# All products of 512 moving columns issued as two products of 256 columns each, bank half by bank half

## The reference

```python
def first_block(x, mem, ...):
    x = x + 0.5 * swiglu(rms_norm(x, ffn1_norm[l]), ffn1_w_in[l], ffn1_w_out[l])
    u = rms_norm(x, mix_norm[l]) @ w_in[l]
    ...
    x = x + mixed @ w_out[l]
    x = x + 0.5 * swiglu(rms_norm(x, ffn2_norm[l]), ffn2_w_in[l], ffn2_w_out[l])

def second_block(x, mem, positions, ...):
    for l in range(DEPTH_2):                 # 2 layers
        h = rms_norm_2(x, ffn1_norm_pre[l])
        x = x + 0.5 * rms_norm_2(swiglu_2(h, ffn1_w_in[l], ffn1_w_out[l]), ffn1_norm_post[l])
        h = rms_norm_2(x, mix_norm_pre[l])
        y = token_mixer(h, mem, cos, sin, ...)
        x = x + rms_norm_2(y, mix_norm_post[l])
        h = rms_norm_2(x, ffn2_norm_pre[l])
        x = x + 0.5 * rms_norm_2(swiglu_2(h, ffn2_w_in[l], ffn2_w_out[l]), ffn2_norm_post[l])
    return x
```

## Time and profile before

| | |
|---|---|
| runs | 1740.83 us median (1740.42 to 1740.84) |
| profiled execution | 1740.77 us, its span 1739.0 us |
| TensorE (PE) | busy 1729.4 us, 99%, 12568 matmuls |
| weight loads (PEld) | 1586.5 us, 91%, 12568 |
| VectorE (DVE) | 1074.9 us, 62% |
| ScalarE (ACT) | 920.5 us, 53% |
| granted TensorE clock | full, mean 1.000 |
| DMA | 189 GB/s mean |

### The profile page before, as it was taken

How to read it: one execution, slowest core, us unless ns; L and a number is a source line. 1 busy time by engine, 2 the same in 40 slices (tenths; PEclk the granted TensorE clock), 3 DMA queues, 4 the chain that set the end, 5 groups by cost and what they waited for, 6 DMA issues and landing times.

```text
span 1739.0 us, 31193 instructions
## 1 busy us (share of the span) xinstructions
PE 1729.4 (99%) x12568; PEld 1586.5 (91%) x12568; DVE 1074.9 (62%) x1516; ACT 920.5 (53%) x1265; POOL 34.4 (2%) x60
## 2 busy tenths in 40 slices
PE   9999999999999999999999999999999999999998
PEld 9999888999999999898898999899999888989997
DVE  6555787655655566556686555755584566775555
ACT  6444677444454445576746444644464576664443
POOL 0000120000000000000000000000000000000000
PEclk9999999999999999999999999999999999999999
DMA  8655524655665555553355555655555543446552
GB/s 326 244 193 193 182 109 148 227 186 196 221 228 193 187 181 200 179 212 143 122 194 188 194 190 198 231 208 195 190 201 183 194 171 128 164 157 220 192 193 96
DMA packets 47551, 328.58 MB, mean 189 GB/s; under 512 B 5488, under 2 KB 5744, under 8 KB 9072
## 3 DMA queue, kind: packets, MB, share of 16 engines
q1 hardware_dynamic: 44640, 316.93, 50.4%
q10 hardware_dynamic: 2832, 10.54, 1.7%
HBM read 326.39 MB, written 1.05 MB: 188 GB/s over the span
## 4 chain that ended last, share of the span: by engine, by line
PE 95%; ACT 2%; DVE 1%; issue 1%; DMA 0%; POOL 0%; SPq 0%; DVEq 0%; POOLq 0%; ACTq 0%
PE work L1764 19%; PE work L1766 19%; PE work L1765 19%; PE acc L1766 8%; PE acc L1765 8%; PE acc L1764 8%; PE work L2004 4%; PE work L1873 3%; PE acc L2088 1%; PE acc L2070 1%; ACT hi L664 1%; ACT prob L858 1%; PE acc L2080 1%; DVE lo L1170 1%; DMA xT_raw<-xT 0%
## 5 line engine op out<-in xcount | busy, mean ns | idle before, releaser
L1170 DVE TENSOR_TENSOR lo<-raw,hi 128x2048 fp32r<-128x2048 f32 x271 | 620.3, 2291 | 318.1 <-ACT hi L664 317.7
L664 ACT ACTIVATE hi<-raw 128x2048 fp32r<-128x2048 f32 x271 | 518.9, 1915 | 376.9 <-PE work L1766 349.8
L1764 PE MATMUL work<-xT_hi,hi 128*128 128x256 f32 x2464 | 685.4, 278 | 1.2 <-ACT merge L848 0.7
L1766 PE MATMUL work<-xT_hi,lo 128*128 128x256 f32 x2464 | 681.0, 276 | 0.0
L1765 PE MATMUL work<-xT_lo,hi 128*128 128x256 f32 x2464 | 681.0, 276 | 0.0
L1764 PEld LDWEIGHTS work<-xT_hi,hi 128*128 128x128 f32 x2464 | 462.5, 188 | 10.6 <-issue 6.9
L1765 PEld LDWEIGHTS work<-xT_lo,hi 128*128 128x128 f32 x2464 | 463.0, 188 | 2.4
L1766 PEld LDWEIGHTS work<-xT_hi,lo 128*128 128x128 f32 x2464 | 462.6, 188 | 0.0
L1766 PE MATMUL acc<-hi,hT_lo 128*128 128x512 f32 x480 | 189.2, 394 | 0.0
L1765 PE MATMUL acc<-lo,hT_hi 128*128 128x512 f32 x480 | 188.3, 392 | 0.0
L1764 PE MATMUL acc<-hi,hT_hi 128*128 128x512 f32 x480 | 186.6, 389 | 0.0
(11 more groups left out here) (327 smaller groups left out, 2088.7 us busy)
## 6 DMA issues: line engine op xcount, KB each, us to landing
raw<-stream SPq DMA_DIRECT2D x297, 1024.0 KB, 4.8
mem_in<-mem ACTq DMA_DIRECT2D x3, 1024.0 KB, 5.1
post<-post ACTq DMA_DIRECT2D x6, 512.0 KB, 4.6
memT_raw<-mem2T ACTq DMA_DIRECT2D x2, 1024.0 KB, 7.4
xT_raw<-xT SPq DMA_DIRECT2D x2, 512.0 KB, 5.7
raw<-stream SPq DMA_DIRECT2D x2, 512.0 KB, 6.9
x<-x SPq DMA_DIRECT2D x2, 512.0 KB, 10.9
memT_raw<-mem1T ACTq DMA_DIRECT2D x1, 1024.0 KB, 10.8
```

The source lines that it names most:

```text
L664: nc.scalar.activation(dst, raw[:, s, :], ACT.Copy).then_inc(hi_ready, 1)
L1170: nc.vector.tensor_tensor(lo[:, s, :], raw[:, s, :], hi[:, s, :].bitcast(F32), ALU.subtract).then_inc(lo_ready, 1)
L1764: nc.tensor.matmul(dst, a_hi, b_hi, start=start, stop=False)
L1766: return nc.tensor.matmul(dst, a_lo, b_hi, start=False, stop=stop)
```

## The change

`wide_product` issues a product of 512 columns as two calls of `product` on 256 columns each, first the left half of the bank with all its three matmuls, then the right half. `rows_half` and `out_tile` call it. `tile_products` issues each of its matmuls twice, once for each half. The start flag is on the first matmul of the left half alone and the stop flag on the last of the right half.

```diff
+            def wide_product(dst, a_hi, a_lo, b_hi, b_lo, start, stop):
+
+                for h in range(2):
+                    piece = slice(T * h, T * h + T)
+                    last = product(dst[:, piece], a_hi, a_lo, b_hi[:, piece], b_lo[:, piece], start and h == 0, stop and h == 1)
+                return last
+
...
-                    last = product(dst, a_hi[:, kt, P * i:P * i + P], a_lo[:, kt, P * i:P * i + P],
+                    last = wide_product(dst, a_hi[:, kt, P * i:P * i + P], a_lo[:, kt, P * i:P * i + P],
...
-                        last = nc.tensor.matmul(work[:, i, :], a[:, 4 * half + q, P * i:P * i + P], w[:, s, 512 * q:512 * q + 512],
-                                                start=(half, turn, q) == (0, 0, 0), stop=(half, turn, q) == (1, 2, 3))
+                        for c in range(2):
+                            at = 512 * q + T * c
+                            last = nc.tensor.matmul(work[:, i, T * c:T * c + T], a[:, 4 * half + q, P * i:P * i + P], w[:, s, at:at + T],
+                                                    start=(half, turn, q, c) == (0, 0, 0, 0), stop=(half, turn, q, c) == (1, 2, 3, 1))
...
-                            last = product(acc[:, 2 * i + c, :], h[0][:, f, P * i:P * i + P], h[1][:, f, P * i:P * i + P],
+                            last = wide_product(acc[:, 2 * i + c, :], h[0][:, f, P * i:P * i + P], h[1][:, f, P * i:P * i + P],
```

## The result

The changed kernel takes **1757.95 us** (median of five runs, 1757.83 to 1760.33) against 1740.53 us (five runs) for the kernel before: a ratio of 1.0106, 95% interval 1.0095 to 1.0117, so 17.4 us slower. The profiled execution is one of 1757.83 us with a span of 1756.0.

What follows compares the result with a forecast made beforehand. TensorE's own distances between matmul starts were taken as the bound. Two slow bodies +11.2, other pairs -4.2, switches -1.8, the first body's slow stretch gone -0.5: +4.7 us on 1740.8, so 1745.5, range 1732.5 to 1764.

Steps and rivals of the forecast that it cites:

- five bodies that are slow from end to end: Rival: new spacing ahead of feed-forward entries catches five of the six bodies, 1764 us, the range's top; no separate chance.
- four slow bodies: Rival: new spacing ahead of feed-forward entries catches four of the six bodies, 6.2 us each, 1758; no separate chance.
- Fast rhythm: At all 2544 split matmuls: two fast halves take 226.7 ns for 228.8, so -2.1 ns each.
- Switches: Behind 59 stretches of 512s, the switch back to 256 columns disappears, 0.03 us each: -1.8 us.
- Slow rhythm: In feed-forward bodies: without 512-to-256 switches, a body entered slowly stays slow, costing 5.6 us; two such bodies, +11.2 us.
- A round that turns fast at a turn of chunks: Sign in the changed kernel's trace that the forecast is wrong: a slow entry turning fast between chunks.
- two slow bodies: Second feed-forwards of both layers slow throughout, +11.2 us; at least two such bodies had chance 0.40.
- Which body is entered slowly: Behind transposes, the second feed-forwards of both layers are entered slowly, the very first body fast.
- The slow rhythm does not carry: Rival: the turn from output products to the next chunk ends slowness; 1733 to 1735, chance 0.40 including no body caught.
- The fixed price per matmul: Rival: each of 2544 output products pays 15.5 ns twice, 39 us more, 1780; fixed prices together had chance 0.06.
- the estimate of 1747: Rule of columns / 2.4 plus 2.5 ns per matmul at every split: change costs 6.4 us; fixed prices together 0.06.
- The load: Loading 128 columns of weights takes 107 ns, leaving a half product no slack to hide it; used in no number.

Runs made afterwards that it cites:

- experiment 1: Against the kernel before, only the feed-forwards' output products are halved, the other products by token stay whole: 1756.8 us, ratio 1.0088.
- experiments 7 and 8: Changed kernel with each halved product's three matmuls in another order: 1756.8 us; changed kernel with the right half ahead of the left: 1756.5 us.
- experiment 9: Changed kernel with each loop round reordered to half a chunk, one output tile, the other half, the other tile: 1757.7 us, ratio 1.0097.
- experiment 4: Changed kernel, but the first product of each group of output or by-token products stays at 512 columns: 1758.7 us, ratio 1.0106.
- experiment 6: Changed kernel with all activations moved up by 256 bytes in SBUF: 1758.1 us, ratio 1.0098.
- experiment 11: Changed kernel, but the next chunk's first channel product is issued ahead of this chunk's last output product: 1755.0 us, ratio 1.0077.

## Why the prediction was right in direction and short in size

The forecast was +4.7 us, the measured change +17.4. The direction was right, but barely forecast (0.46 for slower, 0.40 for faster by more), and that the range reached to 1764 was luck: it was drawn for up to five bodies that are slow from end to end, and no body is. Nor does the price that it names for four slow bodies, 1758, stand for anything that happened.

1. *Fast rhythm, -2.1 ns a pair:* right. The new halves of a fast round run at 113.5 ns; their being streamed from the weights' buffers costs nothing.
2. *Switches, -1.8 us:* right in kind, large in size. In the kernel before, the distances behind one of the 57 turns add up to 24 ns more than the rhythm behind it, 1.4 us in all. Now the 31 turns from slow to fast still cost 11 ns each and the 26 others 2: 0.4 us stay, and the gain is 1.0.
3. *Slow rhythm:* the forecast took from the trace that the slow rhythm exists, costs 4.5 ns a matmul, is entered behind transposes and was ended by the turns behind 512s, and that the change takes these ends away. That holds, and gives the sign. The step that failed is the next: "I expect a body entered slowly to stay slow", and, unsaid, one entered fast to stay fast. The turn did not become harmless when its 512 went. It flips the rhythm either way, so about half of all rounds are slow in **every** body, where the sum had all rounds of two bodies. A round that turns fast at a turn of chunks is the sign that the prediction itself named for being wrong here. Its two slow bodies are 2784 slow distances, +12.5 us; the trace has 3854 more than before in the bodies, +17.3 us. And it has 1422 more outside them, +6.4 us, where the prediction put no slow stretch at all: the mixers' stretches by token, whose 512s became halves, are often entered slowly as well, behind transposes and behind other small matmuls. That term, at nothing without a reason, is the second thing that failed.
4. *Which body is entered slowly* was forecast wrongly: slow the fourth and the sixth, fast the others. Measured, the first three are entered slowly and the last three fast. Two of them, the second body and the sixth:

```profile
311.49 2.05 PE L2013 MATMUL work<-xT_lo,hi 128*128 128x256 f32 x16
313.38 2.05 PE L2013 MATMUL work<-xT_hi,lo 128*128 128x256 f32 x16
...
1585.38 1.98 PE L2013 MATMUL work<-xT_lo,hi 128*128 128x256 f32 x16
1587.19 1.98 PE L2013 MATMUL work<-xT_hi,lo 128*128 128x256 f32 x16
```

16 matmuls take 1.89 us in the one, 1.81 in the other. It hardly mattered: with flips, the entry only decides whether the odd or the even rounds are slow.
5. *Rivals.* "The slow rhythm does not carry" is half true, and for the reason given there: the turn itself ends it. Its price, 1733, was wrong, because the same turn starts it again. That a fast stretch could turn slow without a transpose was in no case. The fixed price per matmul (1780) fell with the fast rounds. So did the estimate of 1747 from the Trainium skill (TensorE: Matmul & The Clock Gate, Back-to-back issue gap), whose columns / 2.4 plus 2.5 ns, which the section gives for isolated matmuls, makes 109.2 ns of 256 columns and the pair dearer than the 512. The trace has 113.5 ns in fast rounds and 117.8 in slow rounds, and the pair costs less or more by rhythm.
6. *The load.* The prediction took loads that come every 113 ns as agreement with a rule for how long one lasts. The profile records 188 ns for each, and loads that overlap one another (three in a row start at 319.85, 319.96 and 320.08 in the kernel before, 0.19 us each). So these rows neither confirm the rule nor deny it, and no run here shows what slack a load has behind a half. No number of the forecast used it.

In the trace before, the one clue was in plain sight and unused: the 512s' distances go 226, 229, 232 in turn, and all 57 turns stand behind one of 230 ns or more. They could not show what a turn behind an exact 226.7 would do.

Open: what in the array or its load path has the two rhythms. The experiments say what flips them, not why. They also don't say why only the turn from streaming weights to streaming activations does so, nor what in it counts: the moving operand, the stationary one, or both.

## What to carry to other kernels

Where every matmul of 256 columns brings its own weight load, read the distance between starts, and read it in more than one place: it can have two stable values 4% apart, and edits far off may choose between them. Splitting a 512 in two gains 2 ns when the fast one holds and loses 7 when the slow one does, so longer matmuls are worth keeping where the stream changes from one kind of operand to the other. Before an edit removes something regular (here, the 512s at every turn), ask what else that regularity was doing.

## What the runs showed of the hardware

- The dense products' matmuls of 256 columns, with a load each, start every 113.3 or 117.8 ns, those of 512 every 228.8 or 233.2 ns, at one granted clock (mean 0.999 to 1.000 in every trace), with nothing waited for.
- A stretch keeps its value over hundreds of matmuls: 408 matmuls in a row in the fast rhythm in the changed kernel, 335 in the slow rhythm in experiment 1.
- A turn from streaming weights to streaming activations flips it when halves stand ahead of it: 57 of 57 turns in the changed kernel and in experiments 7 and 8, 105 of 105 in experiment 9, 56 of 57 in experiment 4 and likewise in experiment 6 (one slow stretch stayed slow). Behind a 512 it ends slow where the last distance is 226 or 227 ns, and fast where it is longer. The opposite turn flipped nothing in any kernel, as far as it can be read: in experiment 11, 54 of the 117 stand too close to a turn to tell.
